# A two-layer decoder step on one core: three landing buffers for the weight slabs in place of two, and a ring of 8 in place of 16 for the sample tokens' gelu values

## What is computed

```
def trunk(x, ...):
    for i in range(2):
        xn = rmsnorm(x, norm_mix[i])
        y = recurrent_mixer(xn, ...) if i == 0 else conformer_mixer(xn, ...)
        x = x + y
        x = x + peer(rmsnorm(x, norm_ffn[i]), w_q[i], sub_keys[i], u[i], v[i])
    return rmsnorm(x, norm_final), ...

def peer(xn, w_q, sub_keys, u_tab, v_tab):        # 16384 experts, 8 heads, 16 picks each
    q = xt @ w_q
    s = einsum('thpc,hpkc->thpk', q, sub_keys)
    sv, si = top_k(s, 16)                         # 2 x 16 of 128 keys, then 16 of 256 pairs
    best, pos = top_k(cand, 16)
    g = softmax(best)
    act = gelu(einsum('ted,td->te', u_tab[eidx], xblk))
    return einsum('te,ted->td', g * act, v_tab[eidx])
```

## Time and profile before

| what | value |
| --- | --- |
| median of 3 runs | 2171.46 us (2166.41 to 2171.79) |
| the profiled execution's own time | 2170.59 us |
| its span, first to last instruction | 2168.8 us |
| PE busy | 2079.0 us (96%) |
| DVE busy | 1639.0 us (76%) |
| ACT busy | 964.7 us (44%) |
| POOL busy | 334.1 us (15%) |
| mean rate of the DMAs | 165 GB/s |

### The profile page before, as it was taken

How to read it: one execution, slowest core, us unless ns; L and a number is a source line. 1 busy time by engine, 2 the same in 40 slices (tenths; PEclk the granted TensorE clock), 3 DMA queues, 4 the chain that set the end, 5 groups by cost and what they waited for, 6 DMA issues and landing times.

```text
span 2168.8 us, 40396 instructions
## 1 busy us (share of the span) xinstructions
PE 2079.0 (96%) x16458; PEld 1895.1 (87%) x16458; DVE 1639.0 (76%) x3068; ACT 964.7 (44%) x1642; POOL 334.1 (15%) x245
## 2 busy tenths in 40 slices
PE   8999999999999999979998999999999999999988
PEld 7899989999899987767897999999998899877766
DVE  7887995556877778757699779965658876888666
ACT  5654453434433433334655544534344433333344
POOL 0013000000000075332110050000000000656310
PEclk9999999999999999999999999999999999999999
DMA  5343544444544557776431434544445544567763
GB/s 174 108 155 124 169 156 154 152 157 159 175 162 142 159 180 236 245 253 203 136 92 61 141 127 153 168 147 151 155 151 176 167 149 144 166 230 257 246 210 117
DMA packets 112935, 358.34 MB, mean 165 GB/s; under 512 B 17264, under 2 KB 27760, under 8 KB 112496
## 3 DMA queue, kind: packets, MB, share of 16 engines
q1 hardware_dynamic: 99888, 319.99, 45.7%
q0 software_dynamic: 12288, 33.60, 4.8%
q10 hardware_dynamic: 576, 2.18, 0.2%
HBM read 349.09 MB, written 6.63 MB: 164 GB/s over the span
## 4 chain that ended last, share of the span: by engine, by line
PE 52%; DVE 23%; DMA 16%; ACT 6%; issue 2%; POOL 0%; SPq 0%; DVEq 0%; ACTq 0%
DMA land<-stream_dram 16%; PE ps L878 11%; PE ps L879 10%; PE ps L880 10%; DVE w_lo L1470 8%; ACT w_hi L583 5%; PE ps L909 5%; PE ps L911 5%; PE ps L910 5%; PE ps L956 4%; DVE work L1356 1%; DVE work L1592 1%; DVE work L1597 1%; DVE hidden L1671 1%; DVE hidden L1356 1%
## 5 line engine op out<-in xcount | busy, mean ns | idle before, releaser
L1470 DVE TENSOR_TENSOR w_lo<-land,w_hi 128x1024 fp32r<-128x1024 f32 x562 | 686.6, 1222 | 362.5 <-ACT w_hi L583 360.0
L583 ACT CAST w_hi<-land 128x1024 fp32r<-128x1024 f32 x592 | 621.2, 1049 | 620.7 <-DMA land<-stream_dram 575.8
L878 PE MATMUL ps<-act_hi,w_hi 128*128 128x288 f32 x2688 | 810.6, 302 | 19.9 <-DVE act_lo L1196 6.2
L879 PE MATMUL ps<-act_hi,w_lo 128*128 128x288 f32 x2688 | 795.5, 296 | 0.0
L880 PE MATMUL ps<-act_lo,w_hi 128*128 128x288 f32 x2688 | 792.7, 295 | 0.0
L878 PEld LDWEIGHTS ps<-act_hi,w_hi 128*128 128x128 f32 x2688 | 506.2, 188 | 28.0 <-issue 16.8
L880 PEld LDWEIGHTS ps<-act_lo,w_hi 128*128 128x128 f32 x2688 | 508.4, 189 | 0.0
L879 PEld LDWEIGHTS ps<-act_hi,w_lo 128*128 128x128 f32 x2688 | 507.5, 189 | 0.8
L909 PE MATMUL ps<-w_hi,g_hi 128*128 128x512 f32 x1024 | 411.5, 402 | 29.1 <-DVE g_lo L1745 29.0
L910 PE MATMUL ps<-w_lo,g_hi 128*128 128x512 f32 x1024 | 402.6, 393 | 0.0
L911 PE MATMUL ps<-w_hi,g_lo 128*128 128x512 f32 x1024 | 402.3, 393 | 0.0
(11 more groups left out here) (214 smaller groups left out, 1351.6 us busy)
## 6 DMA issues: line engine op xcount, KB each, us to landing
land<-stream_dram SPq DMA_DIRECT2D x592, 512.0 KB
act_d<-smp_stage SPq DMA_DIRECT2D x64, 64.0 KB, 3.3
hidden<-stream_dram,smp_idx POOLq DMA_INDIRECT x128, 4.9
x<-x_dram SPq DMA_DIRECT2D x4, 288.0 KB, 5.3
y_t_dram<-hidden SPq DMA_DIRECT2D x8, 144.0 KB, 1.9
work<-keys_dram SPq DMA_DIRECT2D x1, 1024.0 KB, 7.6
smp_act<-act_d,smp_idx POOLq DMA_INDIRECT x64
work<-keys_dram ACTq DMA_DIRECT2D x1, 1024.0 KB, 6.2
```

Of the source, the lines that this page charges most:

```text
L583: nc.scalar.copy(w_hi[:, m, :], land[:, n % LANDS, :]).then_inc(w_hi_ready, 1)
L878: nc.tensor.matmul(out, w_hi[:, slot, wsl], hi, start=start, stop=False)
L879: nc.tensor.matmul(out, w_lo[:, slot, wsl], hi, start=False, stop=False)
L1470: V.tensor_tensor(w_lo[:, k, :], land[:, n % LANDS, :], w_hi[:, k, :].bitcast(F32), ALU.subtract).then_inc(lo_by_dve, 1)
```

## The change

Three constants. `LANDS` is 3: a third landing buffer and a third `landed` semaphore, and SP's DMA for slab n waits for the split of slab n - 3. `STAGE` is 8: the ring `smp_stage` has 8 tiles, so 2 groups in place of 4, each with its semaphore. `STORE_LAG` is 7: the store of a group follows the DMA of the slab 7 after the last of the group. The landing buffers take 4 KB more in each partition, the ring 1 KB less.

```
-LANDS = 2
+LANDS = 3
...
-STAGE, GROUP = 16, 4
+STAGE, GROUP = 8, 4
 RINGS = STAGE // GROUP
-STORE_LAG = 8
+STORE_LAG = 7
```

## The result

| | before | after |
| --- | --- | --- |
| median | 2170.28 us (2166.41 to 2171.79) | 2098.03 us (2096.93 to 2098.75) |
| the profiled execution | 2170.59 us | 2098.75 us |
| its span | 2168.8 us | 2096.9 us |

The medians are of four runs each. The ratio is 0.9669, with a 95% interval of 0.9653 to 0.9686: 72 us faster. The prediction said 2130, with a range from 2112 to 2157: the sign and the place were right, the size was not. Even the rival "more", 2102, gave too little.

The account below looks back on a forecast made before the run. PE was taken as the bound, busy 2079.0 of 2168.8 us, with late V visits held by two landing buffers. Gains of 30 + 4 + 7 = 41 us gave 2129.6, forecast as 2130 us, range 2112 to 2157.

Parts of the forecast that it names:

- more: Rival, chance 0.05: every wait and each lower clock goes, 44.5 + 11.5 + 13 = 69 us, giving 2102 us.
- The loop through two landing buffers: Late V stage, slabs 244 to 285: 7.1 us for two slabs where PE wants 5.44; third buffer gains 30 of 44.5 us.
- Ring and lag: Ring of 8 and lag of 7: stores have less time but stay hidden by five slabs of PE's work, 0 us.
- the start: Slab 2 is asked for without a wait; PE there waits for DVE's evacuations, so 0, within 1 us each way.
- the price of a late landing: Late V stage, slabs 244 to 285: 9 us kept back, a third of the 42 visits late by 0.6 us.
- the burst: Layer 0's late V stage: loads of the keys and the convolution state, for which 5 us were kept back.
- Two engines at 91% that wait for each other will not both reach 57: Slabs 226 to 243: PE and DVE cannot both reach their floor, so 4 us gained, bounds 0 and 11.5.
- The routing: Slabs 46 to 78: DMAs go out one piece of routing earlier; 7 us of PE's 11.2 gained, bounds 0 and 13.
- No change: Rival, chance 0.09: DVE's order itself makes `g_lo` late, or two buffers fit already; 2167 to 2171 us.
- The landings stretch: Rival, chance 0.22: with three DMAs in the air beside the gathers each landing takes 6.5 us; 2153 us.
- Slower: Rival, chance 0.05: the ring's stores land late behind three slabs' packets in SP's queue, and ACT waits; 2192 us.

Follow-up runs that it names:

- both loads moved: Kernel after, with the load of the next layer's keys issued at slab 284 and that of the convolution state at slab 290: 2095.36 us, ratio 0.9664.
- The early part alone: Kernel after, with the third landing buffer used only below slab 200 of each layer and two slabs in hand from there on: 2154.98 us, ratio 0.9931.
- small adds: Kernel before, with 62 of the 64 adds of the sample's rows working on 32 of 1024 columns: 2165.17 us, ratio 0.998.
- without the gathers: The 64 pairs of gathers of v rows left out: 2135.38 us from the kernel before (two buffers), 2096.54 us from the kernel after (three).
- the ring alone: Kernel before with only the ring of 8 tiles and the store lag of 7, still two landing buffers: 2172.27 us, ratio 1.0008.
- extra traffic: Kernel after, plus a 256 KB DRAM to DRAM copy behind each slab's DMA from 244 to 285: 2107.27 us, ratio 0.9736.

## Why the prediction was wrong in size

**The mechanism held.** The loop through two landing buffers was the pace, the budget of a landing became 5.9 us (5.82 from issue to cast where PE releases the cast), the clock is 1.00, the DMA share is 0.82 and 0.79 where 0.85 was expected, ACT's waits for landings went from 82.4 to 19.4, PE's before L909 to 3.6, and those of L878 for `smp_stage` to nothing. Ring and lag were 0, the start was 0.

**The step that failed is the price of a late landing:** "I expect landings between 4.8 and 5.9 and some visits late still. I keep 9 us for them." The first half came true. With three buffers the landings took 5.08 and 4.67 us on the mean, and 8 and 3 of 42 took more than 5.9; 11 and 7 came after PE had freed the slot. But a cast that begins late isn't yet a PE that waits. In layer 1 these 7 came up to 1.1 us late, with both loads moved some came 1.4 us late, and PE waited for none: layer 1 took 115.8 us against a floor of 115.7. The prediction had worked out a slack of 1.2 us behind the cast ("T' + 1.5, and PE needs it at T' + 2.72") and then priced a lateness of 0.6 us, half of that slack, in full. Those 9 us should have been none. The 1.2 us are for a turn with an add; a turn without one has 1.2 more. That this slack is what swallows the lateness fits these numbers, but no run takes it away to show it. Of the "5 us" kept for the burst 3.2 were right: there the landings of slabs 270 and 271 came 5.2 us late, and PE did wait.

**"Two engines at 91% that wait for each other will not both reach 57"** failed too: 11.0 us came where 4 were taken. It is a rule of thumb about engines, put where a budget was wanted. In layer 0's window before, all 18 of ACT's casts waited for their landing, 40.2 us in total, and DVE for 6.2 us for casts: it stood waiting for casts that waited for landings. With a slab more in hand it is busy for 56.5 of 57.4.

**The routing** was a middle between bounds, 7 between 0 and 13. It gave 13.2, the upper bound. The early part alone shows that it is the third buffer's; DVE's waits for casts in its splits fell from 6.3 and 5.5 us to 1.7 in each layer, over like windows. Why the middle was too low wasn't tested by itself.

**Stages left out:** slabs 24 to 39 and 200 to 225 gave 7.6 us. Their windows are only 1 to 3 us above what they take now, and I had looked only at stages with a large wait in the list of PE's waits.

Together: 11.2 + 7.0 + 6.2 + 7.6 = 32 us more than the sum of 41, less 1 in the rest: the 31 us between 41 and 72.

**The rivals.** "No change" fell twice: small adds show that DVE's order isn't the cause, and without the gathers two buffers still lose. The Trainium skill (DMA: Bandwidth & Descriptors, Anatomy of one DMA) gives its fit for DMAs that GpSimd issues; the prediction used it for slabs, which SP issues, and came to an estimate of 3.2 us. The runs show 3.38 us from issue to cast without the gathers in layer 1, near it, and 4.03 to 4.38 beside them. The advice of the Trainium skill to double-buffer (Trainium Kernel Development and Optimization, Best Practices), so that DMA and compute overlap, isn't enough here: 3.3% of the time lay in the third buffer. "The landings stretch" was half right: they did, by 0.7 us in each layer, but to 5.1 and 4.7 us and not to 6.5. "Slower" by the ring's stores fell with the ring alone. "More" at 2102 was the nearest; it was given 0.05 since each term in it seemed a best case, but one cause, the second buffer's loop, stood behind all of them.

**What stays open:** a fourth landing buffer wasn't tried, nor three with a ring of 16 tiles. By the windows on the floor I would expect neither to bring anything but the burst's 3 us. Why the burst costs 3 us rather than the 2.6 us of PE's two waits wasn't pursued.

## What to carry to other kernels

Find the loop first: with b buffers, one slab passes in (issue to landing + the work that frees the buffer) / b, and a buffer more pays only if that is longer than the consumer's time for a slab. Take issue to landing, as a mean over the stage, and not issue to use: the latter holds the wait for the consumer, and a sum made of it gives back any stage, whatever bounds it. Expect the landings to grow when one more is in the air, here by 0.7 us. Then ask how late a landing may be before the consumer waits, and price only what is later than that. If the new loop is clearly shorter than the consumer's time, take the whole excess over the floor, stage by stage, small ones and lower clocks included, and keep a part back only where a burst or a bound of its own has a row to show for it.

## What the runs showed of the hardware

- The DMA engines delivered 278 GB/s at a share of 0.82 with slabs and gathers mixed, and PE waited for none of it outside the burst. At 337 and 350 GB/s, shares of 0.91 and 0.94, the mean from issue to cast was 6.3 us. I hadn't expected a share of 0.82 to leave the landings in time.
- The mean time from issue to landing of a 512 KB slab grew with the share, in layer 1's windows: 3.35 us at 0.54 and at 0.57 (no gathers, two and three buffers), 4.01 at 0.71 (before), 4.67 at 0.79 (after), 5.85 at 0.91 (extra traffic).
- The kernel before differs from chip to chip and run to run, 2162.24 and 2163.00 us on two chips and 2170.96 and 2171.26 on two others, while the kernel after took 2098.03 and 2097.82 on two chips. That would fit a loop that passes on how long its landings take, against one that PE paces; it wasn't tested.
- A wait of 2.06 us of PE before slab 270 was followed by no lower clock, and one of 3.14 us at 1127.36 us (before L967, at a border of blocks) by a stretch of 3.4 us at half the clock, 1.2 of the two levels 1.2 and 2.4 GHz:

```profile
1128.70:1132.10 3.40, 3.40 (x10) 2.68 (x9) 3.40 (x7) 3.40 (x13) 0.74 (x2) 0.50 0.28 99
```
